# The head of a two-block program on one core: x loaded in three parts, scaled x passed through PSUM, first subtractions moved ahead of the angles

## What is computed

```python
def _rmsnorm(x, g):
    xf = x.astype(jnp.float32)
    y = xf * lax.rsqrt(jnp.mean(xf * xf, axis=-1, keepdims=True) + EPS)
    return (y * g.astype(jnp.float32)).astype(x.dtype)
...
    inv_freq = 1.0 / (ROPE_THETA ** (jnp.arange(0, MLA_ROPE_DIM, 2, dtype=jnp.float32) / MLA_ROPE_DIM))
    ang = positions.astype(jnp.float32)[..., None] * inv_freq
    return jnp.cos(ang), jnp.sin(ang)
...
    for l in range(DEPTH):
        h = _rmsnorm(x, g_mix[l])
        p = h @ w_in[l].astype(h.dtype)
        c_q = _rmsnorm(p[..., :o1], g_q[l])
...
        y_attn = _mla_attention(q_nope, q_rope, k_nope, k_rope, v)
...
        x = x + y
        h2 = _rmsnorm(x, g_ffn[l])
        z = _dwconv(h2 @ w_up[l].astype(h2.dtype), w_dw_ffn[l], b_dw_ffn[l])
        zg, zv = jnp.split(z, 2, axis=-1)
        x = x + (jax.nn.silu(zg) * zv) @ w_down[l].astype(h2.dtype)
    return _rmsnorm(x, g_final)
```

## Time and profile before

| | us |
|---|---|
| median of 3 runs | 2860.53 |
| lowest, highest | 2849.62, 2862.86 |
| the profiled execution | 2854.44 |
| its span in the trace | 2852.4 |
| mean granted clock of TensorE in it | 0.989 of full |

### The profile page before, as it was taken

The page is one execution under the profiler, slowest core; times in us unless marked ns, Lnnn a source line. Parts: engine busy times, 40 slices in busy tenths (PEclk is TensorE's granted clock), DMA queues, the critical chain, the costliest instruction groups (busy, mean ns, idle before and its releaser), DMA issues.

```text
span 2852.4 us, 37491 instructions
## 1 busy us (share of the span) xinstructions
PE 2757.5 (97%) x13506; PEld 2240.8 (79%) x13506; DVE 1747.6 (61%) x1983; ACT 788.5 (28%) x1305; POOL 1736.9 (61%) x984
## 2 busy tenths in 40 slices
PE   8899999999999999999998999999999999999999
PEld 6778888888777888877776778888877777788887
DVE  6885766426877666256777558054567785832635
ACT  3433322102443222024565222011223331310202
POOL 5784666665966666655443548666474444666664
PEclk9999999999999999999999999999999999999999
DMA  4101222232112222222121223222231111222221
GB/s 150 67 30 61 95 96 100 100 111 82 38 38 95 96 96 96 104 89 78 65 74 52 75 71 113 97 96 96 74 109 60 67 61 58 89 96 97 100 94 65
DMA packets 66484, 237.45 MB, mean 83 GB/s; under 512 B 7264, under 2 KB 7520, under 8 KB 66336
## 3 DMA queue, kind: packets, MB, share of 16 engines
q1 hardware_dynamic: 65504, 234.00, 23.2%
q10 hardware_dynamic: 832, 1.51, 0.2%
HBM read 233.38 MB, written 2.10 MB: 83 GB/s over the span
## 4 chain that ended last, share of the span: by engine, by line
PE 83%; DVE 8%; DVEq 3%; issue 3%; ACT 1%; POOL 1%; ACTq 0%; DMA 0%; SPq 0%; POOLq 0%
PE ps L478 25%; PE ps L481 24%; PE ps L484 24%; PE ps L1157 1%; PE ps L641 1%; DVE ps L1827 1%; PE ps L1009 1%; PE ps L1199 1%; PE ps L1001 1%; PE ps L1004 1%; PE ps L882 1%; PE ps L961 0%; DVEq L1946 0%; DVE qf L1928 0%; DVE negmax L1939 0%
## 5 line engine op out<-in xcount | busy, mean ns | idle before, releaser
L413 POOL TENSOR_SCALAR w_hi<-w_raw 128x1024 fp32r<-128x1024 f32 x437 | 484.7, 1109 | 1061.2 <-PE ps L478 978.6
L415 POOL TENSOR_TENSOR w_lo<-w_raw,w_hi 128x1024 fp32r<-128x1024 f32 x437 | 1102.6, 2523 | 36.5
L478 PE MATMUL ps<-x_hi,w_hi 128*128 128x512 f32 x1864 | 743.8, 399 | 21.3 <-DVE x_lo L1699 5.4
L481 PE MATMUL ps<-x_lo,w_hi 128*128 128x512 f32 x1864 | 729.8, 391 | 0.0
L484 PE MATMUL ps<-x_hi,w_lo 128*128 128x512 f32 x1864 | 729.1, 391 | 0.0
L478 PEld LDWEIGHTS ps<-x_hi,w_hi 128*128 128x128 f32 x1864 | 352.3, 189 | 106.8 <-issue 11.8
L484 PEld LDWEIGHTS ps<-x_hi,w_lo 128*128 128x128 f32 x1864 | 352.3, 189 | 75.1
L481 PEld LDWEIGHTS ps<-x_lo,w_hi 128*128 128x128 f32 x1864 | 352.4, 189 | 74.7 <-issue 4.1
L478 PE MATMUL ps<-a_hi,w_hi 128*128 128x512 f32 x512 | 200.0, 391 | 0.0
L484 PE MATMUL ps<-a_hi,w_lo 128*128 128x512 f32 x512 | 199.2, 389 | 0.0
L481 PE MATMUL ps<-a_lo,w_hi 128*128 128x512 f32 x512 | 199.2, 389 | 0.0
(11 more groups left out here) (430 smaller groups left out, 4623.3 us busy)
## 6 DMA issues: line engine op xcount, KB each, us to landing
w_raw<-wts SPq DMA_DIRECT2D x437, 512.0 KB, 3.4
xres<-xT SPq DMA_DIRECT2D x2, 1024.0 KB, 8.4
outT<-xres SPq DMA_DIRECT2D x8, 256.0 KB, 2.0
pf<-pT ACTq DMA_DIRECT2D x2, 512.0 KB, 4.7
prm<-prm SPq DMA_DIRECT2D x1, 452.0 KB, 4.1
lev<-levels ACTq DMA_DIRECT2D x1, 384.0 KB, 3.6
wtmp<-pos SPq DMA_DIRECT2D x1, 128.0 KB, 2.9
ident<-identity SPq DMA_DIRECT2D x1, 64.0 KB, 9.9
```

The costliest lines, as they stand in the source:

```text
L413: nc.gpsimd.tensor_scalar(w_hi[:, s, :], w_raw[:, s, :], 1.0, 0.0, ALU.mult, ALU.add).then_inc(w_rounded[s], 1)
L415: nc.gpsimd.tensor_tensor(w_lo[:, s, :], w_raw[:, s, :], w_hi[:, s, :].bitcast(F32), ALU.subtract).then_inc(w_split[s], 1)
L478: mm = nc.tensor.matmul(out, whi, xhi, start=first, stop=False)
L481: mm = nc.tensor.matmul(out, whi, xlo, start=False, stop=False)
```

## The change

Five edits, all in the head of the program.

1. SyncE no longer loads the parameters as one transfer in second place. ScalarE's queue issues the two pieces that the head needs (24 and 3 columns). SyncE waits for the positions and these two (`s_prm` at 48) after it has issued x, the first two weight blocks and the identity; then it issues the other 877 columns and after them weight blocks 2 and 3. ScalarE and VectorE wait for the rest (`s_prm` at 80) ahead of the loop over the layers.
2. x comes as tiles 0 and 1, then 2 and 3, then 4 to 7, between the first weights. The last part shares `s_id` with the identity, so whoever waits for it waits for both; the later thresholds of `s_id` go up by 16.
3. ScalarE writes x times gain to one of the PSUM banks 4, 6 and 7 as well, ahead of the rounding (16 instructions for 8 tiles instead of 8), and VectorE subtracts `x_hi` from that bank (`split_first`) instead of working it out again from `xres`. From tile 3 on ScalarE waits until the bank it wants has been read. The squares of tiles 0 and 1 move behind all the roundings.
4. VectorE subtracts tiles 0 and 1 ahead of the last five angle steps; the other six stay behind them.
5. TensorE does the first four steps of block 0, then the first four of block 1, then the rest in turns, where it did three of block 0, two of block 1 and so on. The warm-up is six matmuls instead of eight.

```diff
+X_BANK = [4, 6, 7]
...
-IN_STEPS = ([(0, 0), (0, 1), (0, 2), (1, 0), (1, 1), (0, 3), (1, 2), (1, 3)]
+IN_STEPS = ([(t, kt) for t in (0, 1) for kt in range(4)]
             + [(t, kt) for kt in range(4, KD) for t in (0, 1)] + [(t, kt) for t in range(2, W_IN) for kt in range(KD)])
...
             sp.dma_start(wtmp[64:128, :].bitcast(I32), pos_d.to_broadcast([64, S])).then_inc(s_prm, 16)
-            sp.dma_start(prm[:, :, 0], prm_d).then_inc(s_prm, 16)
-            sp.dma_start(xres[:, 0:4, :], x_in[:, 0:4, :]).then_inc(s_x, 16)
+            sp.dma_start(xres[:, 0:2, :], x_in[:, 0:2, :]).then_inc(s_x, 16)
             sp.dma_start(w_raw[:, 0, :], wts[0]).then_inc(w_loaded[0], 16)
-            sp.dma_start(xres[:, 4:8, :], x_in[:, 4:8, :]).then_inc(s_p, 16)
+            sp.dma_start(xres[:, 2:4, :], x_in[:, 2:4, :]).then_inc(s_p, 16)
             sp.dma_start(w_raw[:, 1, :], wts[1]).then_inc(w_loaded[1], 16)
+            sp.dma_start(xres[:, 4:8, :], x_in[:, 4:8, :]).then_inc(s_id, 16)
             sp.dma_start(ident[:, :], ident_d).then_inc(s_id, 16)
+            sp.wait_ge(s_prm, 48)
+            sp.dma_start(prm[:, PL:C_INVF, 0], prm_d[:, PL:C_INVF]).then_inc(s_prm, 16)
+            sp.dma_start(prm[:, C_DTB:, 0], prm_d[:, C_DTB:]).then_inc(s_prm, 16)
...
-            idle(5, 8)
+            idle(5, 6)
...
-                        pe.wait_ge(s_id, 16)
+                        pe.wait_ge(s_id, 32)
...
-            act.wait_ge(s_prm, 32)
+            def scaled_and_rounded(m):
+
+                if m >= 3:
+                    act.wait_ge(x_split, m - 2)
+                nc.scalar.activation(ps[X_BANK[m % 3]][:, :], xres[:, m, :], ACT.Identity, bias=0.0, scale=prm[:, GN + m, :])
+                rounded(m, prm[:, GN + m, :])
+
+            nc.scalar.dma_start(prm[:, 0:PL, 0], prm_d[:, 0:PL]).then_inc(s_prm, 16)
+            nc.scalar.dma_start(prm[:, C_INVF:C_DTB, 0], prm_d[:, C_INVF:C_DTB]).then_inc(s_prm, 16)
+            act.wait_ge(s_prm, 48)
             act.wait_ge(s_x, 16)
-            for m in range(4):
-                rounded(m, prm[:, GN + m, :])
+            for m in range(2):
+                scaled_and_rounded(m)
+            act.wait_ge(s_p, 16)
+            for m in range(2, 4):
+                scaled_and_rounded(m)
+            act.wait_ge(s_id, 32)
+            for m in range(4, KD):
+                scaled_and_rounded(m)
             for m in range(2):
                 nc.scalar.activation(sq[:, m, :], xres[:, m, :], ACT.Square).then_inc(x_sq, 1)
-            act.wait_ge(s_p, 16)
-            for m in range(4, KD):
-                rounded(m, prm[:, GN + m, :])
             act.wait_ge(ang_ready, 1)
...
+            def split_first(m):
+
+                dve.wait_ge(x_round, m + 1)
+                V.tensor_tensor(x_lo[:, m, :], ps[X_BANK[m % 3]][:, :], x_hi[:, m, :].bitcast(F32), ALU.subtract).then_inc(x_split, 1)
...
-            dve.wait_ge(s_prm, 32)
+            dve.wait_ge(s_prm, 48)
...
+            split_first(0)
+            split_first(1)
             for c in (c1, c2, c3):
...
-            dve.wait_ge(s_x, 16)
-            for m in range(4):
-                split_x(m, m, prm[:, GN + m, :])
-            dve.wait_ge(s_p, 16)
-            for m in range(4, KD):
-                split_x(m, m, prm[:, GN + m, :])
+            for m in range(2, KD):
+                split_first(m)
```

More of the change, by code:

```diff
@@ L1256, in _ @@
                 square(m, m, xres[:, m, :])
+            act.wait_ge(s_prm, 80)
             with act.Fori(0, DEPTH) as l:
@@ L1776, in _ @@
             V.tensor_scalar(rope_cs[r, :], rope_cs[r, :], prm[r, C_SG, :], None, ALU.mult)
+            dve.wait_ge(s_prm, 80)
             with dve.Fori(0, DEPTH) as l:
@@ L2245, in _ @@
             V.tensor_tensor(w_t[:, :, :], w_t[:, :, :], dtT[:, :, :], ALU.mult).then_inc(small_dve, 1)
-            dve.wait_ge(s_id, 32)
+            dve.wait_ge(s_id, 48)
             def pair(g, p):
@@ L2494, in _ @@
             V.tensor_scalar(lbt[:, 0, :], lbt[:, 2, :], -1.0, None, ALU.mult)
-            dve.wait_ge(s_id, 48)
+            dve.wait_ge(s_id, 64)
             dve.drain()
```

## The result

| | us |
|---|---|
| before, median (16 runs) | 2854.33 (2849.62 to 2862.86) |
| after, median (16 runs) | 2863.81 (2861.40 to 2867.65) |
| ratio | 1.0032, 95% interval 1.0026 to 1.0039 |
| the profiled execution before, its span | 2854.44, 2852.4 |
| the profiled execution after, its span | 2865.14, 2863.3 |

The change makes the program slower by 0.32%, about 9 us. That is less than the 0.5% named ahead, and the time lies inside the range; but with 16 runs on each side the interval excludes both no change and the small gain that was forecast. The head itself came out as predicted. Here it is, with the rows that answer to those of before.

What follows compares the result with a forecast made beforehand. TensorE, 97% busy, was taken as the bound, so only its loss at the start, ahead of the row sum (L508), could be gained. 2856.9 - 0.3 = 2856.6, about 2857 us; range 2848 to 2864.

Steps and rivals of the forecast that it cites:

- The sum of the head: Start of the row sum (L508) at 31.3 to 31.9 instead of 31.92 us: -0.6 to 0, taken as -0.3.
- The port argument: In the head, VectorE's two-SBUF or fast single-input instructions wait until GpSimd's end; those reading PSUM do not.
- the bounds of 0.60 and 0.70: ScalarE's two instructions per x tile: 0.64 us each assumed, bounds 0.60 and 0.70, worth 0.4 us either way.
- From L508 on: Behind the row sum, the root, factor row and all that follows were claimed to keep their distances.
- The term for everything behind L508: Everything after the row sum was assumed to keep its distances, so no gain or loss was added there.
- The base: Starting time for the whole kernel: 2856.9 us, mean of all four executions, chosen over the median of three timed runs.
- The chances for more than 0.5% either way: Whole kernel faster or slower by over 0.5% (14 us): chances 0.04 and 0.03.
- (1): Rival: VectorE's angle steps in the head are not held by GpSimd; -2.9 us, so 2854; chance 0.17.
- (2): Rival: TensorE's new wait at L508 lowers its clock; +1.1 us, so 2858; chance 0.17.
- (3): Rival: small parameters land near 10 us, delaying the head's angle steps; +3.4 us, so 2860; chance 0.08.
- (4): Rival: block 0's gain is wholly waited away, nothing visible; together with the forecast, within 0.6 us, chance 0.55.
- something not listed: Any cause outside the forecast and its rivals, no place or size given; chance 0.03.

Runs made afterwards that it cites:

- b_dve_cut: Kernel before without VectorE's two waits for the halves of x ahead of the subtractions: 2860.98 us, ratio 1.0017.
- a_delay3: Changed kernel with three extra 480-column PSUM writes on VectorE, a drain behind each, ahead of the sum-of-squares signal: 2857.82 us, ratio 1.0005.
- a_delay: Changed kernel with one extra 480-column PSUM write (0.46 us) on VectorE ahead of the sum-of-squares signal: 2854.30 us, ratio 0.9994.
- a_delay2: Changed kernel with two extra 480-column PSUM writes on VectorE, a drain behind each, ahead of the sum-of-squares signal: 2857.10 us, ratio 1.0009.
- a_act2: Changed kernel with two more one-column activations and drains on ScalarE ahead of squares 2 to 7, VectorE's code untouched: 2864.09 us, ratio 1.0023.
- a_dve_pad1: Changed kernel with one tiny memset and drain in VectorE's idle time ahead of the first moved subtraction: 2855.30 us, ratio 0.9991.
- a_qpsum: Changed kernel with the rotated query kept in its PSUM bank and q_lo made from there: 2849.79 us, ratio 0.9977.
- b_qpsum: Kernel before with the rotated query kept in its PSUM bank and q_lo made from there: 2845.91 us, ratio 0.9960.

## Why the prediction was wrong

**The head was right, step by step.** Forecast against measured: the first parameter step at 4, 4.33; x tiles 0 and 1 at 5.6, 5.94; weights 0 at 7.4, 7.22; tile 4 of ScalarE at 13.2, 12.75; the two first weight splittings and the first real matmul at 10.9, 10.85; the three L1778 steps ending at 15.65, 15.46; ScalarE's tile 5 held until 17.45, 17.28; tile 7 rounded at 21.35, 21.07; the root's table loaded at 25.9, 25.56; TensorE in front of the row sum at 30.1, 30.69, since block 2 started at 29.17 and not at 28.75; L508 at 31.3 to 31.9, 31.30. The wait there was 0.61 instead of 1.2 to 1.7. The sum of the head was taken as -0.3 and is -0.6, within its bounds. The port argument held: three angle steps took 4.91 us beside GpSimd, and no subtraction from PSUM was held. Writing to PSUM took 0.67 where writing to SBUF took 0.70; the instructions to either started 0.61 us apart, within the bounds of 0.60 and 0.70. The Trainium skill, "ScalarE: Activation LUTs", "Step-by-step: what each stage is for", calls PSUM the faster of the two to write to; the trace agrees by 0.03 us in the length of one, but at the same spacing it bought no time.

**The step that failed** is a half-sentence in the part on what bounds the kernel: "From L508 on, the root, the factor row and all that follows keep their distances". They did for 80 us. Then idle times that go with the place of VectorE's code, 0.05 us longer ahead of 163 us and 0.35 us longer ahead of 201 us, turned meetings of VectorE and GpSimd, and the distances changed by some 3 us in the first layer and 5 in the second. The term for everything behind L508 was put at nothing; by medians it was a loss of about 9 us, of which the place alone, in b_dve_cut, gives 0.17%, 4 to 5 us. That such meetings exist could be seen in the trace of before, the cost of the place could not: of the 16 `q_lo` some took 0.68 and one 1.97, so this loop was full of meetings that could end either way. I looked at the head alone and treated 99% of the span as stiff.

**The base was off as well.** I took 2856.9, the mean of four executions; 16 executions have a median of 2854.33. With that base the forecast would have been 2854.0, and the miss is 10 us, not 7. The chances for more than 0.5% either way were right in kind, since the change did not move the time by as much. The range was cut unevenly: by its own terms it goes from 2847.5 to 2867.0, and the stated upper end of 2864 contains the measured 2863.81 by luck, as no term in it stood for what happened.

**The rivals.** (1), VectorE slipping through: no; it was held as in the forecast. (2), clock lost behind L508: not in after, whose wait was too short; where it waited 1.86, 1.90 and 2.50 us (a_delay3, a_delay, a_delay2) the clock did fall to half at 34 us, and where it waited 1.77 (a_act2) it did not. So such a fall does occur, but those three kernels are at 1.0005, 0.9994 and 1.0009, and no loss of this kind can be seen in them. (3), the small parameters late: no, 4.33. (4), nothing to be seen: no. The true cause was not on the list; it went under "something not listed", at 0.03. a_dve_pad1 shows what the change does with VectorE's code at its old place: 0.9991, interval 0.9982 to 1.0000, which takes in the forecast's gain of 0.3 us near its edge; its middle is a gain of 2.6 us. At the other places but -2 the changed kernel stands at 0.9994 to 1.0010, so that a gain of the head by itself is not shown.

## What to carry to other kernels

When an edit is worth less than a microsecond, look first for instructions whose duration varies in the trace of before though their work is the same: each is a meeting that a shift of hundredths of a microsecond can turn, and here their sum (6 us) was ten times the edit. Take such an instruction out of the shared way (here by letting one input come from PSUM) before tuning anything ahead of it. Even then the place of the code can be worth more than the edit (a_qpsum and b_qpsum are 3.9 us apart). And when a delay cures a loss, move the code without the delay, and delay without moving the code, before believing in the delay.

## What the runs showed of the hardware

- VectorE's subtraction with two SBUF inputs and GpSimd's tap with two inputs, started within 0.07 us of each other: with GpSimd 0.02 us or more ahead (by the profile) it ran in 1.28 to 1.29 and VectorE took 1.76 to 1.82; with GpSimd at most 0.01 us ahead VectorE ran in 0.68 or 0.69 and GpSimd took 1.81 to 1.83. With `w_lo` 0.02 to 0.06 us ahead the subtraction took 2.86 to 2.91; in three meetings with leads of 0.01 to 0.02 us VectorE still came first.
- Two instructions less in VectorE's code, ahead of a loop, made a program of 2857 us slower by 0.17% (interval 0.07% to 0.28%), and nothing else was edited. The visible marks are an idle time of 0.5 us that stays at its place in the code while the instructions move past it, and in the loop idle times of 0.22 instead of 0.17 us and of 0.50 instead of 0.145. The Trainium skill, "Vector Engine (DVE) Microarchitecture Reference", "Instruction fetch and dispatch (NX sequencer)", describes how each instruction is taken from the engine's own memory ahead of its dispatch; no run here shows whether the idle times arise there.
- The same was not seen on ScalarE: 14 instructions more changed nothing (1.0002).
